# First mixing branch of a two-block transformer kernel: the head norms of both token tiles moved behind all four chunks

## The reference, cut to what matters

```
def rwkv7_time_mix(h_rw, mu, w0, w2, a0, a2, g2, k_k, k_a, r_k, gn_g, gn_b):
    ...
    def step(S, inp):
        r_t, k_t, v_t, d_t, a_t, b_t = inp
        sa = jnp.einsum('bhvk,bhk->bhv', S, a_t)
        S = S * d_t[:, :, None, :] + sa[..., None] * b_t[:, :, None, :] + v_t[..., None] * k_t[:, :, None, :]
        return S, jnp.einsum('bhvk,bhk->bhv', S, r_t)
    ...
    _, y = lax.scan(step, S0, xs)
    y = jnp.moveaxis(y, 0, 1)
    ym = jnp.mean(y, -1, keepdims=True)
    yv = jnp.mean(jnp.square(y - ym), -1, keepdims=True)
    y = ((y - ym) * lax.rsqrt(yv + RW_GN_EPS)).reshape(B, T, RW_WIDTH) * gn_g + gn_b
    bonus = jnp.sum(r * k * r_k, -1, keepdims=True) * v
    return (y + bonus.reshape(B, T, RW_WIDTH)) * g
```

## Time and profile before

| what | value |
|---|---|
| median of three runs | 3236.07 us (3235.59 to 3236.58) |
| profiled execution, its own time | 3236.41 us |
| its span | 3234.6 us |
| PE busy | 3035.9 us (94%) |
| DVE busy | 1772.4 us (55%) |
| ACT busy | 687.6 us (21%) |
| mean granted PE clock | 0.979 of full |

### The profile page before, as it was taken

One profiled execution on the slowest core, in us unless ns is written; L12 is line 12 of the kernel. 1 busy time (PEld: TensorE's weight loads), 2 busy tenths in 40 slices (PEclk: granted clock), 3 DMA queues, 4 the chain that ended last, 5 costly groups with the idle time before them and its releaser, 6 DMA issues. The chain is left out here.

```text
span 3234.6 us, 51790 instructions
## 1 busy us (share of the span) xinstructions
PE 3035.9 (94%) x22322; PEld 2359.5 (73%) x22322; DVE 1772.4 (55%) x2616; ACT 687.6 (21%) x1314; POOL 40.7 (1%) x80
## 2 busy tenths in 40 slices
PE   8999988999998999998889999989999999988998
PEld 8987764549976998674457995555888885555897
DVE  5554555556655564455555566584334663196665
ACT  1102113212112101212311103271111002144210
POOL 1000000000000000000000000000000000000000
PEclk9999999999999999999999999999999999998999
DMA  8645412226645756312216744201223442221442
GB/s 278 224 162 172 147 51 79 79 92 219 213 163 181 240 178 206 130 68 105 79 53 198 250 156 146 78 1 52 79 80 103 143 163 91 88 95 60 153 160 104
DMA packets 279635, 430.29 MB, mean 133 GB/s; under 512 B 9944, under 2 KB 147520, under 8 KB 279408
## 3 DMA queue, kind: packets, MB, share of 16 engines
q1 hardware_dynamic: 273920, 411.52, 37.6%
q0 software_dynamic: 5024, 14.34, 1.4%
q10 hardware_dynamic: 464, 1.12, 0.1%
HBM read 425.91 MB, written 1.05 MB: 132 GB/s over the span
## 5 line engine op out<-in xcount | busy, mean ns | idle before, releaser
L453 PE MATMUL bank<-xT,ring 128*128 128x128 f32 (+3 forms) x4608 | 796.3, 333 | 15.8 <-ACTq L1041 4.7
L453 PE MATMUL bank<-arena 64*64 64x64 f32 (+9 forms) x7244 | 746.9, 283 | 47.0 <-DVEq L3915 8.9
L453 PEld LDWEIGHTS bank<-xT,ring 128*128 128x128 f32 (+1 forms) x4608 | 686.6, 195 | 118.0 <-issue 52.9
L453 PEld LDWEIGHTS bank<-arena 128*128 128x128 f32 (+4 forms) x7244 | 647.8, 164 | 154.3 <-issue 32.4
L453 PE MATMUL bank<-ring,xT 128*128 128x512 f32 (+1 forms) x1344 | 582.7, 585 | 8.9 <-DMA ring<-in_ple_w_gate 4.7
L453 PE MATMUL bank<-ring,arena 128*128 128x256 f32 (+1 forms) x1584 | 443.3, 432 | 17.7 <-DVE arena L846 6.5
L453 PEld LDWEIGHTS bank<-ring,xT 128*128 128x128 f32 x1344 | 251.7, 193 | 276.6 <-issue 264.4
L453 PEld LDWEIGHTS bank<-ring,arena 128*128 128x128 f32 x1584 | 300.9, 192 | 132.6 <-issue 84.5
L789 DVE TENSOR_TENSOR arena<-arena,bank 128x256 f32<-128x256 f32 (+1 forms) x198 | 92.2, 466 | 430.4 <-PE bank L453 291.4
L701 ACT COPY arena<-bank 128x256 f32<-128x256 f32 (+1 forms) x264 | 107.7, 408 | 782.0 <-PE bank L453 781.0
L749 DVE TENSOR_TENSOR arena<-ring,arena 128x1024 f32<-128x1024 f32 (+1 forms) x216 | 257.1, 1190 | 7.4
(11 more groups left out here) (392 smaller groups left out, 2098.4 us busy)
## 6 DMA issues: line engine op xcount, KB each, us to landing
ring<-in_ffn_w SPq DMA_DIRECT2D x88, 1024.0 KB, 8.0
ring<-in_w_in SPq DMA_DIRECT2D x32, 2048.0 KB, 7.8
ring<-in_ffn_w_in SPq DMA_DIRECT2D x44, 1024.0 KB, 6.7
arena<-in_ada_w SPq DMA_DIRECT2D x20, 2048.0 KB, 12.5
ring<-in_ffn_w SPq DMA_DIRECT2D x16, 2048.0 KB, 7.9
ring<-in_ffn_w_out SPq DMA_DIRECT2D x12, 2048.0 KB, 7.9
ring<-in_hgrn_w_in SPq DMA_DIRECT2D x12, 2048.0 KB, 7.8
ring<-in_ffn_w SPq DMA_DIRECT2D x8, 1536.0 KB, 6.8
```

Of the source, the lines that this page charges most:

```text
L453: return self.e.matmul(o, lhsT, rhs, start=start, stop=stop, skip_group_check=True)
```

## The change

DVE's list is written in another order; the other engines' lists stay as they are. The four chunks' steps now stand together, then norm 0, the copy of the turned tile 0, and norm 1. For that the norm is split into four functions with the same instructions in the same order.

```diff
                     ins.then_inc(to_dve.freed, dve.up(to_dve.freed))
                     dve.wait_ge(to_dve.freed, dve.sent(to_dve.freed))
 
+            for tt in range(2):
                 if tt:
                     dve_branch_turned(dve, 0)
-                y = br_tok[:, tt]
-                y3 = y.rearrange("p (h n) -> p h n", h=8)
-                t3 = gn_tmp.rearrange("p (h n) -> p h n", h=8)
-                v.tensor_reduce(small[:, 8:16], y3, AX.X, ALU.add).then_inc(dve_step, dve.up(dve_step))
...
-                dve_head_std(dve, y3, t3, 8, 64, 64e-5)
...
-                v.tensor_tensor(y, y, g_tok[:, tt], ALU.mult).then_inc(branch_ready, dve.up(branch_ready))
-                dve.wait_ge(branch_ready, dve.sent(branch_ready))
+                dve_rwkv_center(dve, tt)
+                dve_rwkv_var(dve, tt)
+                dve_rwkv_scale(dve, tt)
+                dve_rwkv_gate(dve, tt)
+
+        def dve_rwkv_center(dve, tt):
+            v = nc.vector
+            y3, _ = rwkv_heads(tt)
+            v.tensor_reduce(small[:, 8:16], y3, AX.X, ALU.add).then_inc(dve_step, dve.up(dve_step))
...
+        def dve_rwkv_var(dve, tt):
+            y3, t3 = rwkv_heads(tt)
+            dve_head_var(dve, y3, t3, 8, 64, 64e-5)
...
+        def dve_rwkv_gate(dve, tt):
...
+            v.tensor_tensor(y, y, g_tok[:, tt], ALU.mult).then_inc(branch_ready, dve.up(branch_ready))
+            dve.wait_ge(branch_ready, dve.sent(branch_ready))
```

More of the change, by code:

```diff
@@ L1682, in dve_rwkv @@
                     dve.wait_ge(to_dve.freed, dve.sent(to_dve.freed))
+            for tt in range(2):
                 if tt:
                     dve_branch_turned(dve, 0)
-                y = br_tok[:, tt]
-                y3 = y.rearrange("p (h n) -> p h n", h=8)
-                t3 = gn_tmp.rearrange("p (h n) -> p h n", h=8)
-                v.tensor_reduce(small[:, 8:16], y3, AX.X, ALU.add).then_inc(dve_step, dve.up(dve_step))
-                dve.wait_ge(dve_step, dve.sent(dve_step))
-                ins = v.tensor_scalar(small[:, 8:16], small[:, 8:16], 1.0 / 64, None, ALU.mult)
+                dve_rwkv_center(dve, tt)
+                dve_rwkv_var(dve, tt)
+                dve_rwkv_scale(dve, tt)
+                dve_rwkv_gate(dve, tt)
@@ new lines, in rwkv_heads @@
+        def rwkv_heads(tt):
+            return br_tok[:, tt].rearrange("p (h n) -> p h n", h=8), gn_tmp.rearrange("p (h n) -> p h n", h=8)
+        def dve_rwkv_center(dve, tt):
+            v = nc.vector
+            y3, _ = rwkv_heads(tt)
+            v.tensor_reduce(small[:, 8:16], y3, AX.X, ALU.add).then_inc(dve_step, dve.up(dve_step))
+            dve.wait_ge(dve_step, dve.sent(dve_step))
+            ins = v.tensor_scalar(small[:, 8:16], small[:, 8:16], 1.0 / 64, None, ALU.mult)
+            ins.then_inc(dve_step, dve.up(dve_step))
+            dve.wait_ge(dve_step, dve.sent(dve_step))
+            ins = v.tensor_tensor(y3, y3, small[:, 8:16].unsqueeze(2).broadcast_to([P, 8, 64]), ALU.subtract)
+            ins.then_inc(dve_step, dve.up(dve_step))
+            dve.wait_ge(dve_step, dve.sent(dve_step))
@@ L1692, in dve_rwkv, with dve_rwkv_scale @@
+        def dve_rwkv_var(dve, tt):
+            y3, t3 = rwkv_heads(tt)
+            dve_head_var(dve, y3, t3, 8, 64, 64e-5)
+        def dve_rwkv_scale(dve, tt):
+            v = nc.vector
+            y3, _ = rwkv_heads(tt)
+            dve_head_scale(dve, y3, 8, 64)
+            yc = br_tok[:, tt].rearrange("p (c n) -> p c n", c=2)
+            for j, op in enumerate((ALU.mult, ALU.add)):
+                ins = v.tensor_tensor(yc, yc, gnp[:, j:j + 1, 0:256].broadcast_to([P, 2, 256]), op)
                 ins.then_inc(dve_step, dve.up(dve_step))
@@ L1693, in dve_rwkv @@
                 dve.wait_ge(dve_step, dve.sent(dve_step))
-                ins = v.tensor_tensor(y3, y3, small[:, 8:16].unsqueeze(2).broadcast_to([P, 8, 64]), ALU.subtract)
-                ins.then_inc(dve_step, dve.up(dve_step))
-                dve.wait_ge(dve_step, dve.sent(dve_step))
-                dve_head_std(dve, y3, t3, 8, 64, 64e-5)
[L1698 to L1708, removed]
-                v.tensor_tensor(y, y, g_tok[:, tt], ALU.mult).then_inc(branch_ready, dve.up(branch_ready))
@@ L1710, in dve_rwkv @@
-                dve.wait_ge(branch_ready, dve.sent(branch_ready))
+        def dve_rwkv_gate(dve, tt):
+            v = nc.vector
+            y = br_tok[:, tt]
+            _, t3 = rwkv_heads(tt)
+            ins = (v.tensor_tensor(t3, v_tok[:, tt].rearrange("p (h n) -> p h n", h=8),
+                                         bonus[:, 8 * tt:8 * tt + 8].unsqueeze(2).broadcast_to([P, 8, 64]), ALU.mult))
+            ins.then_inc(dve_step, dve.up(dve_step))
+            dve.wait_ge(dve_step, dve.sent(dve_step))
+            v.tensor_tensor(y, y, gn_tmp, ALU.add).then_inc(dve_step, dve.up(dve_step))
+            dve.wait_ge(dve_step, dve.sent(dve_step))
+            v.tensor_tensor(y, y, g_tok[:, tt], ALU.mult).then_inc(branch_ready, dve.up(branch_ready))
+            dve.wait_ge(branch_ready, dve.sent(branch_ready))
```

## The result

The changed kernel takes 3243.55 us (median of 10 runs, 3241.78 to 3246.38) where the kernel before takes 3235.94 us (10 runs, 3234.56 to 3239.97). The ratio is 1.0023 with a 95% interval of 1.0014 to 1.0032: slower by about 7.5 us. In two later sets of 11 runs each, on the chips of those sets, it was 3242.51 us (1.0019, 1.0010 to 1.0027) and 3243.29 us (1.0020, 1.0011 to 1.0029). The forecast was 3238.5 us with a range of 3235.2 to 3242.5, and 0.07 for a loss beyond 0.2%. The time lies outside the range, on the side of rival 1.

What follows compares the result with a forecast made beforehand. PE, busy 94% of the span, bounds the kernel through its stops and low clock. Per layer −7.88 + 8.25 + 0.82 = +1.19 us, two layers +2.4 on 3236.07: 3238.5 us, range 3235.2 to 3242.5.

Steps and rivals of the forecast that it cites:

- rival 1: End of branch: clock stays low through tile 0's products, 2.28 us more in a layer, 3243.0 us; chance 0.10.
- The middle: Chunk (1,0): without norm 0 ahead of its X copy it runs like chunk (0,1), 7.88 us gained per layer.
- The end: Last O copy to turned tile 0's copy: PE's turn waits for norm 0, 11.32 us instead of 3.07, 8.25 lost.
- rival 2: Norm 0 at the end: square root's table loaded in time, norm 8.18 us, layer −0.16, 3235.8 us; chance 0.05.
- Norm 1 and ACT: Behind the turned copy: norm 1 still takes 8.18 us and its square root waits for nothing new on ACT.
- The third bound: Behind PE's restart at the turn: low clock lasts 4.95 us, with 9.74 us kept as the end.
- the other row: Stretch at 1010 us: behind a stop of 4.30 us the clock stayed at 0.50 for 9.74 us.
- The fourth bound: Rest of the program: later clock drops fall otherwise once everything is a microsecond or two late; about 1.5 us either way.
- no change within 0.2%: Whole kernel: time within 0.2% (6.5 us) of before; same 0.90, slower 0.07, faster 0.03.
- The figures made of it: One stop swapped for another, clock's part zero before cover: +2.79 us in a layer, or 1.67 with the 1.12 cover.
- Rival 4: Norm 0 at the end lies beside other work, so the middle's gain stays: 15.8 us less, 3220.3 us; chance 0.03.

Runs made afterwards that it cites:

- bridge: Changed kernel plus one 128x512 matmul in the 0.97 us pause between tile 0's turn and products: 3241.49 us (1.0014); again 3242.5 us beside 3243.29 for the changed kernel.
- 9 matmuls at the end: Changed kernel plus 9 matmuls of 128x512 per layer in PE's stop before the turn of tile 0, result overwritten: 3239.94 us, 1.0009.
- 18 matmuls at the end: Changed kernel plus 18 matmuls of 128x512 per layer before the turn of tile 0, taking 15.6 us and outlasting the stop: 3257.99 us, 1.0066.
- 6 matmuls in the middle: Kernel before plus 6 matmuls of 128x512 per layer in PE's 5.46 us stop in chunk (1,0): 3234.7 us, 0.9994.
- 12 matmuls in the middle: Kernel before plus 12 matmuls of 128x512 per layer in chunk (1,0), 10.57 us of matmuls in a 5.46 us stop: 3243.84 us, 1.0025.
- 4 matmuls: Changed kernel plus 4 matmuls of 128x512 directly behind the last gate matmuls, shortening PE's stop to 4.73 us: 3243.76 us, 1.0021.
- 4 matmuls and bridge: Changed kernel plus 4 matmuls behind the last gate matmuls and one in the pause between turn and products: 3241.83 us, 1.0017.
- table early: Changed kernel plus one small square root on ACT behind the sigmoid of tile 0's gate, loading the table in time: 3241.17 us, 1.0015.
- norm 0 in two halves: Changed kernel with norm 0's first half in DVE's idle stretches of chunk (1,0), its second half behind chunk (1,1): 3229.95 us, 0.9980.
- norm 0 in four pieces: Changed kernel with norm 0 in four pieces, in four idle stretches of DVE in chunks (1,0) and (1,1): 3222.07 us, 0.9956.

## Why the prediction was wrong

Right, by its own steps:
- *The middle*: 7.88 us forecast, 16.08 − 8.19 = 7.89 us in the profile. The wait for the X copy is gone.
- *The end*: norm 0 with 9.53 us (493.64 − 484.12 = 9.52), the wait before the turn ("about 8 us", 8.16), the turn at half rate (1.97). From the last O copy at 483.67 us to the turned copy at 495.79 it is 12.12 us, where 11.32 + 0.82 = 12.14 was the sum. The table load came behind the variance as before, so rival 2 did not occur. The experiment that loads the table early shows that its price was set too high at 1.35 us in a layer: the restart comes sooner by that, but into more low clock, and about half of it is left.
- *Norm 1 and ACT*: the stop for its square root is 0.34 us, nothing new.

Wrong:
- *How long the clock stays low.* The third bound took 4.95 us from the one restart in the same branch, with the reason that the work there was nearer in kind. It was 7.6 and 7.9 us, between that and the other end, 9.74. The restart in the middle is followed by 4.95 us of PE work without a pause; the one at the end by a turn of 2 us, then a pause of 1 us, then the products. That is the pattern of the other row, with a shorter pause. So the likeness that mattered was not the kind of work but whether PE works on behind the restart. The cost: the products lost 2.3 and 2.5 us and not 1.0, the cover of 1.12 us was exceeded by 1.2 and 1.4, and the layers came to +2.1 and +2.3 instead of +1.19. Rival 1 was the right mechanism, at a little under half of its price: it added 2.28 us to a layer, measured were 0.9 and 1.1.
- *Later drops of the clock.* The fourth bound allowed 1.5 us either way, from three runs that lay within 1 us. In the profiled run they made +2.3 us. One profile says little on them: in the first profile of the bridge the whole span is only 0.5 us above before, though its branches are 2.4 above, and in its second profile the span is 7.6 us above with the same branches. And the ten runs of the kernel before lie within 5.4 us. But the medians say that "either way" was wrong too. The table sets the excess of the two layers (PE's start in chunk (1,0) to its start in the products of tile 1, from the profile, against 35.92 and 35.91 us before) beside the excess of the median over the kernel before of the same set.

| kernel | two layers, us | median, us | rest, us |
|---|---|---|---|
| norm 0 between chunks (1,0) and (1,1) | +0.1 | −0.2 | −0.3 |
| changed, three sets | +4.4, +3.5, +4.1 | +7.6, +5.8, +6.7 | +3.2, +2.3, +2.6 |
| 9 matmuls at the end | +0.7 | +3.2 | +2.5 |
| 18 matmuls at the end | +15.1 | +21.6 | +6.5 |
| 6 matmuls in the middle | −4.4 | −2.0 | +2.4 |
| 12 matmuls in the middle | +5.5 | +7.4 | +1.9 |
| bridge, two sets | +2.4, +2.4 | +5.1, +5.9 | +2.7, +3.5 |
| 4 matmuls | +4.3 | +6.9 | +2.6 |
| 4 matmuls and bridge | +1.7 | +5.2 | +3.5 |
| table early | +3.0 | +4.5 | +1.5 |
| norm 0 in two halves | −7.9 | −6.9 | +1.0 |
| norm 0 in four pieces | −15.7 | −14.3 | +1.3 |

The kernel whose layers keep their length has no loss in the rest. Every one that shifts what follows, to a sooner or a later time, loses 1.0 to 3.5 us there, and 6.5 with the largest shift. The layers come from one profile each, and in the changed kernel one layer varied by 1.1 us, but a chance would not fall on one side fourteen times. So a shift away from the kernel before has a cost of its own here, which the prediction's sum had at nothing. Part of it is seen as low clock in untouched lines (564 to 573 us, above); why the kernel before lies so well, and what sets these drops in one execution, is open.

The conclusion "no change within 0.2%" failed by the two together: 2.0 us of the first and 2.3 of the second on a forecast of 2.4 make the 6.7 us of the profiled run. This agrees with the run with four matmuls, where stops of 4.73 and 8.16 us were followed by equally slow products. One fixed amount of time the runs don't show: the clock rose 3.6 to 9.1 us behind the restart. The figures made of it, 1.67 to 2.79 us in a layer, hold the measured 2.11 and 2.31, but by luck: the two stops were not equal for the clock. It cost 2.42 us behind the old one and 0.8 on the turn and 2.3 on the products, 3.1 in all, behind the new one, because the two differ in what comes behind them.

Rival 4, that norm 0's cost could be hidden whole, was rightly given little for this change, and its price of 15.8 us was nearly what the version in four pieces brought (14.3 in the median, 15.7 in its two layers).

## What to carry to other kernels

To take a block of work out of a chain does not help if its new place is on the chain as well; price both places, and look for idle stretches of its own engine that are as long as pieces of it. When the clock falls behind a stop, read what PE does right behind the restart: here a burst of 2 us and a pause of 1 kept it low for longer, and the loss reached the next dense stage. A change that shifts the rest of the program moved the median by 1.0 to 3.5 us beyond what its own stage shows (6.5 with the largest shift), so the stage's rows and the median have to be given side by side.

## What the runs showed of the hardware

- The clock had fallen by the restart, or at most 1.9 us behind it, for stops of 3.2, 4.7, 5.5, 5.9 and 8.2 us alike, and cost the products of tile 0 about as much behind 3.2 us (8.66 and 8.80 us) as in the mildest case behind 8.2 (8.50).
- The moment of the rise is not tied to the restart: with the restart 1.2 us sooner it came no sooner, and one and the same program had it 5.8 us and 7.8 us behind the restart in the two layers of one profile.
- What PE does behind the restart counts: without a pause the clock was back after 3.6 to 5.0 us (ten layers: kernel before, norm 0 between the chunks of tile 1, the three profiles with the bridge), with a pause of 0.97 us behind the turn after 5.3 to 9.1 us (twelve layers).
- Matmuls whose result nobody needs keep the clock at full in the stage behind (at the end: turn 1.15 us instead of 1.97, products 7.11 instead of 9.39). In the middle they gained 2.2 us per layer, 4.4 in all, of which 2.0 reached the median.
